# A hybrid attention and mixture-of-experts layer: the per-layer products moved into the first attention tile, and the extra blocks' tables made in parts inside expert blocks one to six

## The chip, the cores and the metric

The kernel runs on one core of one Trainium2 chip. The metric is the device time of one execution in microseconds (us), lower is better. Times of the kernel before: a median of 1537.45 us over three runs (1536.6 to 1537.8).

## The reference

One decoder layer on 512 tokens of width 1024, all in float32:

```python
h = x
a = rms_norm(h, g_mix);  proj = a @ w_in
o_moba = moba_attention(...)              # 8 heads of 64, causal, blocks of 256
o_gla  = rms_norm(gla_chunked(...), g_gla_norm) * silu(rg)
h = h + concat(o_moba, o_gla) @ w_out
f = rms_norm(h, g_ffn)
h = h + moe_ffn(f, w_router, b_router, w1, b1, w2, b2)   # top 4 of 32 experts
ple = rms_norm(p @ w_ple_proj, g_ple)     # p: 512 x 256, w_ple_proj: 256 x 1024
h = h + sigmoid(h @ w_ple_gate) * ple
return rms_norm(h, g_final)
```

An expert is `clamped_swiglu(x @ w1[e] + b1[e]) @ w2[e] + b2[e]`, with w1[e] 1024 x 2048 and w2[e] 1024 x 1024, so 12 MB of weights for each of 32 experts. `ple` depends on nothing but p and the weights: it can be computed at any time before the last sum.

## The kernel before, in words

Each engine has its own program, written out by hand in the order in which it runs; a program goes on when the semaphores it waits for have been counted up. Four token tiles of 128 (T0 to T3) go through these stages.

1. **Projection** (to about 162 us): `x` is normed and multiplied by w_in.
2. **Attention tiles** (about 162 to 282 us): a loop over t = 0 to 3, written out, with steps j = 0 to 5 for pairs of heads. In a tile PE computes the linear-attention products (L1058, L1106, L1108), the scores (L1070), transposes of the probabilities (L1098), and their product with v (L1082). From tile 1 on, the product with w_out for the tile before (`mix_out`, L1023) is filled in between. ACT does the exponentials (L729), copies the transposed probabilities (`pt_copy`, L737) and squares h for the norm (`h_square`, L745); DVE masks, scales, adds; POOL takes the powers (L571).
3. **Routing** (about 283 to 316 us): `mix_out` for T3, half n=0 and then half n=1, the router's logits (L1042, L1467), each token's four experts, ranks within an expert, the table `row_of` of 96 rows for each expert (L1650), and the gather of the first expert's rows from DRAM (POOL, L583).
4. **Experts**: blocks 0 to 31 of 96 rows, one for each expert, and then as many extra blocks as experts with more than 96 tokens need (their number n is read from a table at run time; in these inputs it is 0, as 31 adds of rows by L600 and 384 weight loads show). A block takes 12 pieces of weights of 1 MB each (k = 0 to 11). For each piece SP loads it into one of six slots (`load_chunk`, L411), ACT rounds it to the upper part (`split_hi`, L782), DVE subtracts that from it to get the lower part (`split_lo`, L1531; both into a ring of four pieces, `HL`), and PE multiplies upper and lower parts in 24 products of 128x512 (`w1_chunk` L1217, `w2_chunk` L1249). `turn_x` (L1205) transposes the gathered rows; ACT and DVE split those too (`split_x` L823, `rest_x` L1527), and w1 cannot begin before. `split_lo` counts up `w_lo`, on which SP waits before it fills the slot again. Piece 6 goes into the slot of piece 0. Block 0 is written out and takes its pieces in the order 0, 1, 2, 3, 8, 6, 7, 9, 10, 11; the others are one loop.
5. **Tail**: the gate product with w_ple_gate, `pleo`, last norm, store.

What the change touches lies in stages 2 to 4:

- **The per-layer products**: `turn_ple` (8 transposes, L1151) and `ple_tile` (L1180: 4 tiles x 2 halves x 2 products of 128x512 in float32, each shown as two matmuls) are issued on PE between the routing and block 0's pieces; ACT squares (L804) and scales (L808) the result from PSUM into `pleo`, POOL takes the power. SP loads their inputs (L461, L462) once seven halves of `mix_out` are done.
- **First weights**: SP loads pieces 0 and 1 right after the second half of w_out (with 2 and 3 at 273 us), ACT's `split_hi` of 0 to 3 stands ahead of `h_square(3)`, DVE's `split_lo(0, 0)` stands in the routing.
- **SP's order in the routing**: the load of piece 6 waits for `w_lo` 1, and behind it in SP's program stand the four loads of b1 (L467). ACT's rounding of b1 (`bb_hi`, L796) waits for these, and ACT's `split_x(0)` stands behind it.
- **Tables**: DVE L1674 to L1710 makes tables for all 53 possible blocks in block 0, PE multiplies them with one-hot rows (`gate_tables`, L1194, 16 products with 74 columns), and the loops of all engines begin with a wait for `tab_ready` and a load of n.

```python
            for k in range(4):
                split_hi(0, k)
            h_square(NT - 1)
            store_f(NT - 1)
```

## Time and profile before

| | |
|---|---|
| median of three runs | 1537.45 us |
| the profiled execution | 1536.28 us |
| its span in the trace | 1534.1 us |
| PE busy | 1494.5 us, 97% of the span |
| DVE busy | 1280.0 us, 83% |
| ACT busy | 1004.8 us, 65% |
| POOL busy | 198.5 us, 13% |
| PE's part of the chain that ended last | 94% |
| mean granted clock of PE | 0.988 |

PE, DVE, ACT, POOL are the engines for matrix products, vectors, activations and general work; SP issues DMAs. A busy PE is not PE at its peak, since matmul ends are modelled. The profiled execution is 1.2 us under the median of the runs.

### The profile page before, as it was taken

To read this page: it belongs to the slowest core of one execution; us is meant where nothing else is said; L and a number is where in the kernel's file an instruction comes from. 1 tells how busy PE (TensorE), PEld (TensorE's weight loads), DVE (VectorE), ACT (ScalarE), POOL (GpSimd) and SP (SyncE) were. 2 spreads that over 40 slices of the span, in tenths; PEclk is the share of its full clock that TensorE was granted. 3 is DMA by queue.
4 is the path that set the end of the run, shared out by engine and by line. 5 is a ranking of instruction groups with operands and counts; after the bars stand their busy time and mean duration, and the time that the engine had idled before them with its cause. 6 is when DMAs were issued, how large, how long until landed. Compare 5 with 4: busy or idle time off the path is not lost.

```text
span 1534.1 us, 20725 instructions
## 1 busy us (share of the span) xinstructions
PE 1494.5 (97%) x7115; PEld 1041.7 (68%) x7115; DVE 1280.0 (83%) x1109; ACT 1004.8 (65%) x919; POOL 198.5 (13%) x148
## 2 busy tenths in 40 slices
PE   7999899999999999999999999999999999999997
PEld 5878555566666666676666666666666666666666
DVE  5322356689999999999999999999999999999974
ACT  5432333457777777777777777777777777777642
POOL 6000000020211111111111121111111111111000
PEclk9999799989999999999999999999999999999999
DMA  5215400459999999999999999999999999999921
GB/s 171 98 67 192 178 15 14 157 188 355 374 393 370 372 376 381 375 379 381 380 382 376 377 377 370 375 372 387 373 384 376 382 381 375 380 376 367 380 100 55
DMA packets 126384, 466.58 MB, mean 304 GB/s; under 512 B 7955, under 2 KB 8518, under 8 KB 126358
## 3 DMA queue, kind: packets, MB, share of 16 engines
q1 hardware_dynamic: 118432, 438.73, 75.5%
q0 software_dynamic: 7312, 25.40, 6.8%
q10 hardware_dynamic: 614, 2.11, 0.3%
q8 instruction: 16, 0.26, 0.1%
q14 instruction: 10, 0.08, 0.0%
HBM read 446.67 MB, written 19.53 MB: 304 GB/s over the span
## 4 chain that ended last, share of the span: by engine, by line
PE 94%; DVE 2%; issue 2%; ACT 2%; DMA 0%; POOL 0%; DVEq 0%; POOLq 0%; ACTq 0%
PE ps L1217 46%; PE ps L1249 23%; PE ps L1004 9%; PE ps L1023 3%; PE ps L1347 2%; PE ps L1205 1%; PE ps L1256 1%; PE ps L1232 1%; PE ps L1180 1%; PE ps L1082 1%; PE ps L1070 1%; PE ps L1098 1%; PE ps L1108 1%; PE ps L1042 0%; DMA b_all<-in_b_router_dram 0%
## 5 line engine op out<-in xcount | busy, mean ns | idle before, releaser
L1531 DVE TENSOR_TENSOR HL<-W,HL 128x2048 fp32r<-128x2048 f32 x384 | 881.7, 2321 | 43.2 <-ACT HL L782 40.5
L782 ACT ACTIVATE HL<-W 128x2048 fp32r<-128x2048 f32 x382 | 731.9, 1917 | 174.7 <-PE ps L1217 100.6
L1217 PE MATMUL ps<-HL,XTh 128*96 128x512 f32 x2048 | 563.5, 397 | 0.5 <-DVE XTl L1527 0.5
L1217 PEld LDWEIGHTS ps<-HL,XTh 128*96 128x96 f32 x2048 | 323.2, 162 | 132.9 <-issue 1.9
L1217 PE MATMUL ps<-HL,XTl 128*96 128x512 f32 x1024 | 319.7, 393 | 0.0
L1249 PE MATMUL ps<-HL,HIDTh 128*96 128x512 f32 x1024 | 280.9, 396 | 1.7 <-DVE HIDTl L1559 1.3
L1249 PEld LDWEIGHTS ps<-HL,HIDTh 128*96 128x96 f32 x1024 | 162.7, 161 | 81.8 <-issue 13.2
L1217 PEld LDWEIGHTS ps<-HL,XTl 128*96 128x96 f32 x1024 | 165.2, 161 | 70.5
L600 POOL DMA_INDIRECT y_sums<-actT,row_of x31 | 60.8, 1962 | 949.4 <-ACT actT L841 949.4
L1249 PE MATMUL ps<-HL,HIDTl 128*96 128x512 f32 x512 | 159.6, 393 | 0.0
L1249 PEld LDWEIGHTS ps<-HL,HIDTl 128*96 128x96 f32 x512 | 82.7, 161 | 35.3
L1392 DVE TENSOR_TENSOR PWl<-wst,PWh 128x1024 fp32r<-128x1024 f32 x24 | 29.0, 1223 | 69.0 <-ACT PWh L667 68.1
L583 POOL DMA_INDIRECT XG<-f_rows,row_of x33 | 83.6, 2534 | 17.3 <-DVE row_of L1650 8.2
L812 ACT ACTIVATE HIDTh<-ps 128x384 fp32r<-128x384 f32 x64 | 31.5, 492 | 61.3 <-PE ps L1256 61.1
L1023 PE MATMUL ps<-wst,actT 128*128 128x512 f32 x128 | 58.9, 603 | 0.0
L673 ACT ACTIVATE W<-ps 128x512 f32<-128x512 f32 x20 | 11.9, 594 | 65.2 <-PE ps L1004 65.2
L729 ACT ACTIVATE M<-M,nmax 128x128 f32<-128x128 f32 (+3 forms) x32 | 18.0, 561 | 46.3 <-DVE nmax L1500 46.2
L1555 DVE TENSOR_TENSOR HIDr<-T,SIG 96x512 f32<-96x512 f32 x64 | 44.0, 688 | 5.0
L1497 DVE SCALAR_TENSOR_TENSOR M<-dist,ps 128x128 f32<-128x128 f32 (+3 forms) x32 | 15.4, 483 | 36.7 <-PE ps L1070 27.9
L817 ACT ACTIVATE SIG<-T 96x512 f32<-96x512 f32 x64 | 40.0, 624 | 9.3 <-DVE T L1543 8.3
L823 ACT ACTIVATE XTh<-ps 128x768 fp32r<-128x768 f32 x32 | 26.0, 813 | 28.3 <-PE ps L1217 26.0
L1543 DVE TENSOR_SCALAR T<-ps 96x512 f32<-96x512 f32 x64 | 43.5, 679 | 1.0 <-PE ps L1217 1.0
(270 smaller groups left out, 1378.8 us busy)
## 6 DMA issues: line engine op xcount, KB each, us to landing
W<-in_w_dram SPq DMA_DIRECT2D x384, 1024.0 KB, 8.3
wst<-in_w_in_dram SPq DMA_DIRECT2D x6, 2048.0 KB, 8.6
H<-in_x_dram SPq DMA_DIRECT2D x8, 512.0 KB, 5.0
wst<-in_w_out_dram SPq DMA_DIRECT2D x2, 2048.0 KB, 10.9
W<-in_w_ple_gate_dram SPq DMA_DIRECT2D x4, 1024.0 KB, 7.7
y_sums<-M SPq DMA_DIRECT2D x1, 2688.0 KB, 15.5
f_rows<-M ACTq DMA_DIRECT2D x4, 512.0 KB, 2.6
out_dram<-TL SPq DMA_DIRECT2D x4, 512.0 KB, 2.6
```

The costliest lines, as they stand in the source:

```text
L583: pool.indirect_dma_start(XG[:], None, f_rows, bass.IndirectOffsetOnAxis(ap=row_of[:, b:b + 1].bitcast(U32), axis=0)).then_inc(xg_in, 16)
L600: pool.indirect_dma_start(y_sums, bass.IndirectOffsetOnAxis(ap=rows.bitcast(U32), axis=0), YR, None, compute_op=ALU.add).then_inc(y_added, 16)
L782: act.activation(HL[:, k % HRING, 0], w_slot(k), ACT.Copy).then_inc(w_hi, 1)
L812: act.activation(HIDTh[:, 4 * h:4 * h + 4], ps[:, 2 * h, 0:4 * CAP].rearrange("p (f j) -> p f j", f=4), ACT.Copy).then_inc(hth_out, 1)
L817: act.activation(SIG[:], T1[:], ACT.Sigmoid, scale=ALPHA).then_inc(sig_done, 1)
L1004: last = pe.matmul(ps[:, g % 4], l, r, start=(c == 0 and m == 0), stop=(c == NC - 1 and m == 2))
L1023: last = pe.matmul(ps[:, bank], actT[:, c, t * P:(t + 1) * P], wst[:, n, c], start=(c == first_c), stop=(c == last_c))
L1217: last = pe.matmul(ps[0:CAP, 2 * h + n], xt[:, c], HL[:, s, part, cc * 1024 + n * 512:cc * 1024 + (n + 1) * 512], start=(h == 0 and c == 0 ...
L1249: last = pe.matmul(ps[0:CAP, 4 + n], ht[:, f], HL[:, s, part, ff * 1024 + n * 512:ff * 1024 + (n + 1) * 512], start=(f == 0 and ht is HIDT ...
L1531: dve.tensor_tensor(HL[:, k % HRING, 1], w_slot(k if ready is None else k - 4), HL[:, k % HRING, 0].bitcast(F32), ALU.subtract).then_inc(w ...
L1543: dve.tensor_scalar(t1, ps[0:CAP, 2 * h:2 * h + 2, 0:512:2], LIMIT, None, ALU.min).then_inc(glu_min, 1)
L1555: dve.tensor_tensor(HIDr[:, h * 512:(h + 1) * 512], T2[:], SIG[:], ALU.mult).then_inc(hid_ready, 1)
```

## The change

The inputs of the per-layer products, and `pleo`, get other places in SBUF: `pleo` takes the first 4096 columns of `W`, which were weight slots 0 and 1, and these slots move to a new area `W01`, which lies over the second half of w_out. So pieces 0 and 1 are loaded once the last tile's product with that half is done; to have it done first, the last tile takes half n=1 before n=0. The products are issued in tile 0, two halves per step. ACT copies them out in tile 0, squares them in tile 1, scales them in tile 2. `gate_tables` covers only the 32 first blocks in block 0; the tables of the extra blocks are made by DVE in six parts, in blocks 1 to 6, written out; PE multiplies them in block 6. The loops of PE, ACT and DVE are cut around block 6 and before block 31, and n is read only there.

```diff
+LATE = 6
-        wpp = wst[:, 0, 0:4, :]...
-        prow = wst[:, 0, 4:6, :]...
-        pT = wst[:, 0, 6:8, :]
-        pleo = wst[:, 1, :, :]...
+        wpp = in_w(18432, 2, D)
+        prow = in_w(20480, NT, PLE)
+        pT = in_w(21504, 2, SEQ)
+        pleo = in_w(0, NT, D)
...
-            return W[:, s * 2048:(s + 1) * 2048] if s < 4 else W45[:, s - 4]
+            return W01[:, s] if s < 2 else W[:, s * 2048:(s + 1) * 2048] if s < 4 else W45[:, s - 4]
...
         def extra_count(eng):
+            eng.wait_ge(tab_ready, 1)
...  (SP)
                 if n == 0:
                     sp.wait_ge(p_lo, 24)
+                    sp.wait_ge(st_ready, 14)
+                    sp.wait_ge(kt_ready, 2)
+                    sp.dma_start(wpp, w_ple_proj[0]...).then_inc(ple_ld, 16)
+                    sp.dma_start(prow, p[0, 0]...).then_inc(ple_ld, 16)
...
-            for k in range(2):
-                load_chunk(sp, 0, k, 0)
             sp.wait_ge(s_done, NT * MH)
             for k in range(2, 4):
                 load_chunk(sp, 0, k, 0)
             sp.wait_ge(wo_done, 2 * NT - 1)
-            sp.dma_start(wpp, ...)
-            sp.dma_start(prow, ...)
+            for k in range(2):
+                load_chunk(sp, 0, k, 0)
             sp.wait_ge(w_lo, 1)
             load_chunk(sp, 0, 6, 0)
             sp.wait_ge(lg_done, NT)
...
-            sp.wait_ge(pp_done, NT)
             for k in range(10, NK):
                 load_chunk(sp, 0, k, 0)
...  (ACT)
+            def ple_out(j):
+                if j == 0:
+                    for c in range(2):
+                        act.wait_ge(pt2_done, c + 1)
+                        act.activation(pT[:, c], ps[:, 3 - c], ACT.Copy).then_inc(pt2_out, 1)
+                else:
+                    for i in (2 * j - 2, 2 * j - 1):
+                        act.wait_ge(pp_done, i + 1)
+                        act.activation(pleo[:, i // 2, ...], ps[:, 3 - i % 2], ACT.Copy).then_inc(pp_out, 1)
...
                         if j < MH // 2:
                             expo(t * MH + i)
+                    if t == 0:
+                        ple_out(j)
                     for i in (2 * j - 2, 2 * j - 1):
                         if j >= 1:
                             pt_copy(t * MH + i)
+                    if t == 1 and j < NT:
+                        ple_square(j)
+                    if t == 2 and j < NT:
+                        ple_scale(j)
...
             with act.Fori(1, 2) as b:
                 expert_block(b, True)
-            act.wait_ge(tab_ready, 1)
+            with act.Fori(2, LATE) as b:
+                expert_block(b)
+            expert_block(LATE, late=True)
+            with act.Fori(LATE + 1, NE - 1) as b:
+                expert_block(b)
             n = extra_count(act)
-            with act.Fori(0, n + (NE - 2)) as i:
-                expert_block(i + 2)
+            with act.Fori(0, n + 1) as i:
+                expert_block(i + (NE - 1))
...  (PE)
+                    if t == 0 and j == 0:
+                        turn_ple()
+                    elif t == 0 and j <= MH // 2:
+                        ple_half(2 * j - 2)
+                        ple_half(2 * j - 1)
...
+            def extra_tables():
+                pe.wait_ge(gate_oh, 1)
+                for a in range(A):
+                    last = pe.matmul(ps[0:CAP, 6, 0:2 * NEXTRA], ohX[:, a, :], tables[:, a, :], ...)
+                last.then_inc(slot_gates, 1)
...  (DVE)
-            split_lo(0, 0)
-            half_turned(T3, 0, 2 * T3 + 1)
-            add_mix(T3, 1, 4)
-            half_turned(T3, 1, 2 * T3 + 2)
+            half_turned(T3, 1, 2 * T3 + 1)
+            add_mix(T3, 0, 4, 2 * T3 + 2)
+            half_turned(T3, 0, 2 * T3 + 2)
...
             dve.wait_ge(x_asked, 1)
+            split_lo(0, 0)
             split_lo(0, 1)
...
+            for b, part in enumerate((extra_experts, taken_blocks, block_tables, slots_hot, extra_pairs, extra_rows)):
+                expert_block(b + 1, part)
+            with dve.Fori(LATE + 1, NE - 1) as b:
+                expert_block(b)
```

Where instructions stand, at three places on which the prediction rests. PE's program in the first attention tile, from its second pair of scores to the second transposes of probabilities: L1070 and L1105 are the scores, L1098 and L1138 the transposes, L1069 and L1080 the per-layer transposes and products, the 64x128 rows and L1108 or L1148 linear attention, the rest the product with v. Before:

```order
L1070 MATMUL ps<-W 128x128 [waits s_masked]
L1070 MATMUL ps<-W 128x128
L1098 MATMUL ps<-ident,M 128x128 [waits p_scaled] x2
L1106 MATMUL ps<-M,W 64x128 [waits a_out]
```

And now:

```order
L1069 MATMUL ps<-ident,W 128x128 [waits ple_ld]
L1069 MATMUL ps<-ident,W 128x128 x7
L1105 MATMUL ps<-W 128x128 [waits s_masked]
L1105 MATMUL ps<-W 128x128
L1080 MATMUL ps<-W 128x512 [waits pt2_out]
L1080 MATMUL ps<-W 128x512 x3
L1138 MATMUL ps<-ident,M 128x128 [waits p_scaled] x2
L1146 MATMUL ps<-M,W 64x128 [waits a_out]
```

Eight transposes and four wide products stand ahead of the first transposes of probabilities; twelve more products stand ahead of the later ones. SP's program from the loads of w_out to b1, before:

```order
L453 DMA wst<-in_w_out_dram 128x8x512
L411 DMA W<-in_w_dram 128x2x1024 x2
L411 DMA W<-in_w_dram 128x2x1024 [waits s_done]
L411 DMA W<-in_w_dram 128x2x1024
L461 DMA wst<-in_w_ple_proj_dram 128x2x1024 [waits wo_done]
L462 DMA wst<-in_p_dram 128x4x256
L411 DMA W<-in_w_dram 128x2x1024 [waits w_lo]
L467 DMA actT<-in_b_dram 32x512 [waits lg_done]
```

And now:

```order
L466 DMA wst<-in_w_out_dram 128x8x512
L418 DMA W<-in_w_dram 128x2x1024 [waits s_done]
L418 DMA W<-in_w_dram 128x2x1024
L418 DMA W<-in_w_dram 128x2x1024 [waits wo_done]
L418 DMA W<-in_w_dram 128x2x1024
L418 DMA W<-in_w_dram 128x2x1024 [waits w_lo]
L478 DMA actT<-in_b_dram 32x512 [waits lg_done]
```

Pieces 0 and 1 now come after pieces 2 and 3, behind the wait for `wo_done`; the loads of b1 still stand behind piece 6 and its wait for `w_lo`. ACT's program there, now (L814 is `split_hi` of pieces 0 to 3, L771 `h_square`, L825 the rounding of b1, L840 `split_x`):

```order
L814 ACTIVATE HL<-W 128x2048 [waits w_slot_in0]
L814 ACTIVATE HL<-W 128x2048 [waits w_slot_in1]
L814 ACTIVATE HL<-W 128x2048 [waits w_slot_in2]
L814 ACTIVATE HL<-W 128x2048 [waits w_slot_in3]
L771 ACTIVATE M,ss<-H 128x1024 [waits f_stored,h_ready]
L775 DMA f_rows<-M 128x1024 [waits f_ready]
L821 ACTIVATE ex<-ex 128x16 [waits e_in]
L823 ACT_TABLE_LOAD
L823 ACTIVATE gcol<-tok 96x1
L825 ACTIVATE BB<-actT 128x512 [waits bias_in]
L840 ACTIVATE XTh<-ps 128x768 [waits xt_done]
```

These rows stand in the same order as before, apart from two copies of the per-layer transposes, which are gone from behind the DMA. And DVE's program, now, from the table `row_of` to block 0's second pieces (L1560 is `split_lo`, L1696 the lower part of b1, L1556 `rest_x`):

```order
L1680 SCALAR_TENSOR_TENSOR row_of<-ps,none 96x32 [waits dve_step]
L1685 TENSOR_REDUCE s<-ex 128x4 [waits e_out]
...
L1560 TENSOR_TENSOR HL<-W,HL 128x2048 [waits w_hi,x_asked,dve_step]
L1560 TENSOR_TENSOR HL<-W,HL 128x2048 [waits w_hi]
L1696 TENSOR_TENSOR BB<-actT,BB 128x512 [waits bb_hi]
L1556 TENSOR_TENSOR XTl<-ps,XTh 128x768 [waits xh_ready]
L1560 TENSOR_TENSOR HL<-W,HL 128x2048 [waits w_hi] x2
```

Before, only one `split_lo` stood between the wait for `x_asked` and the lower part of b1; the one of piece 0, which counts `w_lo` to 1, has moved here from the routing.

## Rows read from the trace of the kernel before

**Rows 1.** The page, part 4: the chain that ended last, share of the span by engine.

```profile
PE 94%; DVE 2%; issue 2%; ACT 2%; DMA 0%; POOL 0%; DVEq 0%; POOLq 0%; ACTq 0%
```

**Rows 2.** Stretches of one block: us, busy of PE, PEld, DVE, ACT, POOL, clock, DMA, GB/s.

```profile
574.28:609.72 35.44, 35.44 (x170) 24.68 (x169) 34.24 (x24) 27.02 (x21) 5.45 (x3) 1.00 1.02 378
1212.20:1247.64 35.44, 35.44 (x170) 24.68 (x169) 33.55 (x24) 26.84 (x21) 4.35 (x2) 1.00 1.02 379
```

**Rows 3.** A stretch of 1 us in the first attention tile, columns as in rows 2.

```profile
166.00:167.00 1.00, 0.12 (x2) 0.00 (x0) 0.78 (x4) 0.32 (x3) 0.00 (x0) 0.50 0.86 352
```

**Rows 4.** Chain of waits: start us, us, what; the first two attention tiles.

```profile
167.73 0.69 PE ps L1098 x2
...
183.92 1.94 PE ps L1058 x8
...
194.82 0.37 PE ps L1106 x4
195.19 0.42 PE ps L1108 x2
```

**Rows 5.** Chain of waits: per-layer products (L1180), first pieces, tables (L1194).

```profile
311.94 3.67 PE ps L1180 x4
...
321.45 2.76 PE ps L1217 x12
324.22 3.63 PE ps L1180 x8
...
330.62 3.43 PE ps L1180 x8
...
343.86 2.70 PE ps L1194 x32
```

**Rows 6.** Timeline of PE, a run of products with 32 columns.

```profile
303.39 1.01 PE L1145 MATMUL ps<-M 128*96 128x32 f32 x10
```

**Rows 7.** Timeline of ACT: start us, us, operation, idle before and releaser.

```profile
208.91 1.06 ACT L745 ACTIVATE M<-H 128x1024 f32<-128x1024 f32 x1
...
318.06 1.02 ACT L804 ACTIVATE wst<-ps 128x1024 f32<-128x1024 f32 x1 [0.94 <-PE ps L1180]
```

**Rows 8.** DMA issues from 273.0 to 273.45, from 273.45 and from 300: us to landing last.

```profile
W<-in_w_dram SPq DMA_DIRECT2D x2, 1024.0 KB, 8.0
...
W<-in_w_dram SPq DMA_DIRECT2D x1, 1024.0 KB, 9.0
...
actT<-in_b_dram SPq DMA_DIRECT2D x4, 64.0 KB, 2.8
```

**Rows 9.** Timeline, all engines, the routing.

```profile
282.94 7.30 ACT L782 ACTIVATE HL<-W 128x2048 fp32r<-128x2048 f32 x4
...
291.65 0.37 SPq L461 DMA_DIRECT2D wst<-in_w_ple_proj_dram  x1
...
300.13 1.06 ACT L745 ACTIVATE M<-H 128x1024 f32<-128x1024 f32 x1 [9.89 <-DVE H L1449]
...
303.59 2.11 SPq L467 DMA_DIRECT2D actT<-in_b_dram  x4
```

**Rows 10.** Timelines of POOL, DVE and PE, from the first gather to block 1.

```profile
310.44 1.11 POOL L583 DMA_INDIRECT XG<-f_rows,row_of  x1 [8.22 <-DVE row_of L1650]
...
312.03 0.17 DVE L1655 TENSOR_REDUCE s<-ex 128x4 f32<-128x16 f32 x1 [1.87 <-ACT ex L792]
...
314.03 2.29 DVE L1531 TENSOR_TENSOR HL<-W,HL 128x2048 fp32r<-128x2048 f32 x1
...
317.15 0.96 DVE L1527 TENSOR_TENSOR XTl<-ps,XTh 128x768 fp32r<-128x768 f32 x1 [0.23 <-ACT XTh L823]
...
323.09 0.86 DVE L1674 TENSOR_TENSOR M<-it_b,xend 128x672 f32<-128x672 f32 x1
...
315.45 0.83 PE L1205 MATMUL ps<-ident,XG 96*128 96x96 f32 x8
...
361.64 1.17 PE L1217 MATMUL ps<-HL,XTh 128*96 128x512 f32 x4 [0.45 <-DVE XTl L1527]
```

More of the change, by code:

```diff
@@ L589, in _ @@
             pool.tensor_tensor(asked[:], tok[0:1, 0:1], tok[0:1, 0:1], ALU.add).then_inc(x_asked, 1)
[L590 to L596 removed]
+            gather(1)
             def add_rows(rows):
@@ L787, in _ @@
             store_f(NT - 1)
-            for c in range(2):
-                act.wait_ge(pt2_done, c + 1)
-                act.activation(pT[:, c], ps[:, 4 + c], ACT.Copy).then_inc(pt2_out, 1)
             act.wait_ge(e_in, 1)
@@ L841, in store_y, with expert_block @@
                     act.activation(YR[:, i * 512:(i + 1) * 512], ps[0:CAP, 4 + i], ACT.Copy, scale=gcol[:]).then_inc(yr_out, 1)
-            def expert_block(b, second=False):
+            def expert_block(b, second=False, late=False):
                 split_hi(b, 0)
@@ L847, in expert_block @@
                 sigmoid(b - 1, 1)
+                if late:
+                    act.wait_ge(slot_gates, 2)
+                    act.activation(slot_gate[:, NE:NBLK + NEXTRA], ps[0:CAP, 6, 0:2 * NEXTRA], ACT.Copy).then_inc(slot_gates_out, 1)
                 split_hi(b, 2)
@@ L1047, in _, with turn_ple, ple_half @@
             pe.wait_ge(consts, 17)
+            def turn_ple():
+                pe.wait_ge(ple_ld, 32)
+                for c in range(2):
+                    for t in range(NT):
+                        last = pe.transpose(ps[:, 3 - c, t * P:(t + 1) * P], prow[:, t, c * P:(c + 1) * P], ident[:])
+                    last.then_inc(pt2_done, 1)
+            def ple_half(i):
+                if i == 0:
+                    pe.wait_ge(pt2_out, 2)
+                elif i >= 2:
+                    pe.wait_ge(pp_out, i - 1)
+                t, n = i // 2, i % 2
+                for c in range(2):
+                    last = pe.matmul(ps[:, 3 - i % 2], pT[:, c, t * P:(t + 1) * P], wpp[:, c, n * 512:(n + 1) * 512],
+                                     start=(c == 0), stop=(c == 1))
+                last.then_inc(pp_done, 1)
             MIX_STEPS = [range(0, 5), range(5, 8), range(8, 13), range(13, 16)] + 2 * [range(0)]
@@ L1147, in slot_tokens @@
                     last.then_inc(tok_done, 1)
-            def turn_ple(c):
-                for t in range(NT):
-                    last = pe.transpose(ps[:, 4 + c, t * P:(t + 1) * P], prow[:, t, c * P:(c + 1) * P], ident[:])
-                last.then_inc(pt2_done, 1)
             pe.wait_ge(oh_ready, 1)
@@ L1199, in gate_tables, with turn_x @@
                 last.then_inc(gt_done, 1)
-            def turn_x(b):
+            def extra_tables():
+                pe.wait_ge(gate_oh, 1)
+                for a in range(A):
+                    last = pe.matmul(ps[0:CAP, 6, 0:2 * NEXTRA], ohX[:, a, :], tables[:, a, :], start=(a == 0), stop=(a == A - 1))
+                last.then_inc(slot_gates, 1)
+            def turn_x(b, late=False):
+                if late:
+                    pe.wait_ge(slot_gates_out, 2)
                 pe.wait_ge(xg_in, b * 16 + 16)
@@ L1581, in expert_block @@
                 split_lo(b, 5)
+                if part is not None:
+                    part()
                 second_half(b)
@@ L1679, in _ @@
-            link(dve.tensor_scalar(tabf[:, NBLK:NBLK + 1], xend[:, NE - 1:NE], 0.0, None, ALU.add))
-            link(dve.tensor_copy(tab[:], tabf[0:1, :]))
-            link(dve.tensor_scalar(full, Jm, CAP - 0.5, None, ALU.is_gt))
-            link(dve.tensor_copy(has, full))
-            for j in range(2, MAXFULL + 1):
-                link(dve.scalar_tensor_tensor(out=full, in0=Jm, scalar=j * CAP - 0.5, in1=full, op0=ALU.is_gt, op1=ALU.add))
-            link(dve.scalar_tensor_tensor(out=Jm, in0=full, scalar=-float(CAP), in1=Jm, op0=ALU.mult, op1=ALU.add))
@@ L1709, in _ @@
-            link(dve.tensor_reduce(own[:], has[:, 0], AX.X, ALU.add))
-            link(dve.tensor_scalar(pair[:, NE:NBLK], tabf[:, NE:NBLK], own[:, 0:1], None, ALU.is_equal))
             split_lo(0, 6)
             clamp(0, 0)
+            dve.wait_ge(slot_gates, 1)
             swiglu(0, 0)
```

216 lines of the change are left out of this document (102 added, 114 removed).

## The prediction, made before the run

> **What bounds the kernel now.** I read the page first: PE holds 94% of the chain that ended last [rows 1]. Then the stretches of one expert block: 35.44 us each, PE busy for all of it at the full clock, DVE for 33.55 to 34.24 us [rows 2]. So the 31 looped blocks run at PE's rate, and DVE has only 1.2 to 1.9 us of room in each. Nothing in the change makes a looped block shorter; what it can win lies before block 1, which begins at 361.64 us [rows 10]. There the chain of waits shows the per-layer products on PE's path: 3.67 us ahead of the first expert's rows, 5.18 us that the chain has between those rows and the first piece at 321.45, and 3.63 and 3.43 us between pieces [rows 5]. The reader is to see that this work fills PE while others are waited for: the first piece of weights is used at 321.45, while the split rows were begun at 317.15 and took 0.96 [rows 10].
>
> **Tile 0 takes the products in.** Sixteen products of 3.43/4 = 0.86 us at the full clock make 13.7 us [rows 5]. Before, this tile is full of short waits, and PE's clock fell to half (1.2 GHz) in it [rows 3]; its last matmul is followed by the next tile at 183.92 [rows 4]. Step by step, now: the eight transposes lie in the wait between the first two pairs of scores. The first product needs ACT's two copies of them (0.6 each), which stand behind two exponentials that end at about 166.1, so it starts at about 167.3, where before the first transposes of probabilities stood (167.73) [rows 4]. From there PE has hardly a wait left: 13.7 us of products; linear attention at the full clock 4 x (0.37 + 0.42) = 3.2 us [rows 4]; other small work at the full clock about 3.4 (an estimate: the rows of tile 0, such as 0.69 for two transposes, at 0.6 of their length); one last copy 0.6. The clock was half when it started; the four products at 311.94, which met the same, took 3.67 instead of 1.71 us, so 2.0 us for that [rows 5]. Sum: 167.3 + 13.7 + 3.2 + 3.4 + 0.6 + 2.0 = 190.2, against 183.9: **+6.3**. The next tile's first products (1.94 us at half clock [rows 4]) then run at the full clock, which gives 1.0 back: **+5.3**. Bounds: +3.3 without any half clock, and +22 if it stays half through the whole tile (17 us more for the products and the rest).
>
> **Tiles 1 and 2.** ACT squares (1.02 plus 0.2 to read the sum) and scales (about 1.1) one tile of the products in each of steps 0 to 3 [rows 7]. Three of four lie where ACT waits for PE. The one of step 3 stands right ahead of `h_square`, which before began with no wait behind `pt_copy` at 208.91 and is on the chain to the next tile [rows 7]: **+1.2 and +1.1**. Bounds: 0, and 9.3 if all eight showed. The power on POOL and the mean on DVE are once for four tiles and hidden.
>
> **The late first weights.** Pieces 0 and 1 used to be in place long before. Now SP issues them where the per-layer inputs were issued, 291.65 [rows 9]. Pieces 2 and 3, the nearest row, issued as a pair like this one, took 8.0 in the median and 9.0 for the second [rows 8]: piece 1 lands at about 292.1 + 9.0 = 301.1. ACT works in its own order, and `split_hi` of pieces 0 to 3 (7.30 for four, so 1.8 each [rows 9]) stands ahead of `h_square(3)`. Pieces 1, 2 and 3 end at 301.1 + 5.4 = 306.5; before, `h_square(3)` started at 300.13, released by DVE [rows 9]. The norm, the last logits, the ranks and the table of rows follow it without slack, so the first gather goes from 310.44 to about 316.8: **+6.4**. Lower bound +4.1, if both landed 5.5 us after 291.65 and all four splits ran then (297.0 + 7.3).
>
> **The wait for b1 behind it.** `split_lo(0, 0)` now follows the gather. Before, the wait for ACT (1.87) stood in DVE's way, and the first split began at 314.03 [rows 10]; without that wait and 6.4 later it is at 318.6, and `w_lo` is 1 at 320.9. Only then does SP issue piece 6 and the four loads of b1, which took 2.11 us to issue and 2.8 to land, at 303.59, long before they were needed [rows 8, 9]. Now they land at about 320.9 + 0.4 + 2.1 + 2.8 = 326.2. ACT's rounding of b1 (0.6) and `split_x` (0.8) and DVE's `rest_x` (0.96 [rows 10]) come behind: PE begins the first piece at about **329.2**, against 321.45 [rows 5]. Were the gather alone in charge, it would be 318.1 + 6.4 = 324.5.
>
> **Block 0.** From the first piece to block 1 it took 361.64 - 321.45 = 40.2 us, PE being busy throughout; without 3.63 and 3.43 of products it is 33.1 [rows 5, 10]. PE will have waited most of the time since the routing when it starts, so 2.0 us for half clock again. `gate_tables` has 32 instead of 74 columns but still 32 matmuls; 32 took 2.70 us, 0.084 each [rows 5], and with 32 columns 10 took 1.01, 0.10 each [rows 6], so I count no gain. Block 1 at 329.2 + 33.1 + 2.0 + 0.1 = 364.4: **+2.8**. DVE, which loses most of its tables here, is no bound; at most piece 8, whose load waits for `w_lo` 3, comes 1 to 2 us late. Lower bound: gather alone in charge, +4.1 for the weights and no half clock: 322.2 + 33.1 = 355.3, -6.3.
>
> The Trainium skill says on the table's width ("TensorE: Matmul & The Clock Gate", LDWEIGHTS) that loading the stationary operand takes its column count over 1.2 GHz, here 96/1.2 = 80 ns whatever the moving width; by it a narrow table and the second table in block 6 each cost 2.6 us, and by columns alone 1.2 and 1.5 us. The trace agrees with the rule (84 ns at 74 columns, 100 at 32), and it speaks against splitting the table in two.
>
> **Blocks 1 to 31.** PE multiplies the extra tables in block 6: the same 32 matmuls, **+2.7** [rows 5], with nothing to hide in, since PE is full. DVE's six parts: the first has an operation of 0.86 [rows 10], a reduction as long and some small ones, 2.6 us as an estimate, and the others 0.5 to 2.2. Room is 1.9 a block, 1.2 while POOL scales the products [rows 2], and DVE is only just ahead when block 1 starts (PE waited 0.45 for it at 361.64 [rows 10]). The first four parts overdraw it by 0.3 to 0.7 each, 2.3 together, of which I put **+1.0** on PE; bounds 0 and 3. The read of n before block 31 and the cut loops: 0, hidden by queued work as at 361.64; at worst 1.
>
> **Sum.** 5.3 + 2.3 + 2.8 + 2.7 + 1.0 = **+14.1 us** on the profiled execution's 1536.3, so 1550.4. The median of the runs stands 1.2 above that execution, so I predict 1551.5 us.
>
> **Rivals.**
>
> 1. *The first expert starts when its rows are there* (faster). If pieces 0 and 1 land so soon, and b1 too, that `h_square(3)` and `split_x(0)` keep their time, PE starts at 318.1 and reaches block 1 at 318.1 + 33.1 = 351.2, -10.4. With tile 0 at its lower bound (+3.3) and block 6 (+2.7) the sum is -4.4: 1533 us. For it: ACT had 9.89 us of waiting ahead of `h_square` [rows 9]. Against: the second piece would have to land by 294.7, 2.6 us after its issue, and nothing of 1 MB did. It decides when what tile 0 to 2 and the blocks cost stays under 10.4. Chance 0.09.
> 2. *The costs fall at their lower ends* (no change). Tile 0 at +3.3, nothing in tiles 1 and 2, block 1 at -4, block 6 +2.7: +2, 1539.5 us. For it: DVE's first block is lighter. Chance 0.08.
> 3. *My forecast.* Late weights and b1 behind `w_lo` take back what the moved products free, and tile 0 pays for them: 1551.5. Chance 0.70.
> 4. *The clock stays half through tile 0.* The bound of +22 instead of +5.3: 1568 us. For it: before, the half clock of 166 us still held when the next tile began at 183.92 [rows 3, 4]. Against: that tile had small products; the wide ones at 311.94 brought the clock up. Chance 0.13.
>
> **How the numbers follow.** A measurement of this kernel tells about 0.2%, 3.1 us, from no change. Faster by more: rival 1, 0.09. Within: rival 2, 0.08. Slower: 0.83. The likeliest is 1551.5. The range goes down to 1541, which leaves out rivals 1 and nearly all of 2, and up to 1564, into rival 4, whose clock may come back late in the tile: the bounds of my own terms (-4 for tiles 0 to 2, -9 for block 0 but not together with them, +3 for DVE) lie within.
>
> **What would show it.** In the trace after: tile 1 starts at 189 to 191 us, not 184, with a half clock that ends within some 4 us of the first product; `h_square(3)` starts 14 us later than 300.13 (7.6 from the tiles, 6.4 from the weights), and the split ahead of it waits for a DMA of weights; ACT waits for the DMA of b1 ahead of `split_x(0)`; the first piece is used at about 337, block 1 at 372; the blocks stay 35.44 us but block 6, which has 2.7 more, and some of 1 to 4. I am wrong if block 1 starts before 361 us, or if looped blocks change their length.

## The result: slower by 28.7 us, twice the forecast

The changed kernel took 1566.3 us (median of 4 runs, 1563.2 to 1566.8), the kernel before in the same comparison 1537.6 (1536.6 to 1539.1): a ratio of 1.0182, 95% interval 1.0164 to 1.0199. The prediction was 1551.5 with a range of 1541 to 1564. The direction was right, the size was not. The span of the profiled execution grew by 30.7, from 1534.1 to 1564.8 us.

**The profile after.** First the page: busy time (part 1), the chain that ended last by engine (part 4) and two groups of part 5.

```profile
PE 1503.3 (96%) x7147; PEld 1046.3 (67%) x7147; DVE 1275.4 (82%) x1102; ACT 1005.9 (64%) x928; POOL 214.2 (14%) x141
...
PE 73%; DVE 3%; issue 1%; DMA 1%; POOL 1%; ACT 1%; SPq 0%; POOLq 0%; ACTq 0%; DVEq 0%
...
L1242 PE MATMUL ps<-HL,XTh 128*96 128x512 f32 x2048 | 566.8, 398 | 12.4 <-DVE XTl L1556 8.2
...
L608 POOL DMA_INDIRECT y_sums<-actT,row_of x31 | 77.6, 2503 | 942.6 <-ACT actT L858 942.6
```

The chain of this profile is followed back to 320.9 us only, and its row adds up to about 80%, so the 73% are not to be set against the 94% of [rows 1]. Three of its pieces (start us, us, what) are new: the landing of b1, an add of POOL's and a gather.

```profile
334.88 5.31 DMA actT<-in_b_dram
...
402.51 10.98 POOL y_sums L608
413.80 10.77 DMA XG<-f_rows,row_of
```

PE is busy for 96% of the span, so the question is where PE stands still or runs slower. The sum by stages is read from PE's and ACT's timelines of both profiles. A block's rows are turned in the block before it, so "rows of block 3" is a mark inside block 2.

| mark | before | after | later by | new |
|---|---|---|---|---|
| tile 0 begins | 162.60 | 166.13 | 3.5 | 3.5 |
| tile 1 begins | 183.85 | 194.07 | 10.2 | 6.7 |
| `h_square(2)` | 278.19 | 290.48 | 12.3 | 2.1 |
| rows of block 2 turned | 370.40 | 387.12 | 16.7 | 4.4 |
| rows of block 3 | 405.82 | 424.62 | 18.8 | 2.1 |
| rows of block 6 | 512.15 | 531.18 | 19.0 | 0.2 |
| rows of block 7 | 547.59 | 575.97 | 28.4 | 9.4 |
| rows of the last block | 1433.59 | 1463.47 | 29.9 | 1.5 |
| end | 1534.1 | 1564.8 | 30.7 | 0.8 |

**Tile 0.** PE's timeline (start us, us, line, operation, count, idle before and releaser), the counterpart of [rows 4]:

```profile
166.13 1.16 PE L1093 MATMUL ps<-W 128*128 128x128 f32 x8 [1.18 <-ACT W L732]
...
170.68 3.70 PE L1080 MATMUL ps<-W 128*128 128x512 f32 x8 [1.32 <-ACT W L751]
...
178.47 3.70 PE L1080 MATMUL ps<-W 128*128 128x512 f32 x8
...
194.07 1.16 PE L1093 MATMUL ps<-W 128*128 128x128 f32 x8
```

Four such groups, 14.8 us of products (14.2 from start to start, as ends are modelled), and between them hardly a wait: PE is the bound of the tile, which takes 27.9 us and not 21.25. The clock, half in this tile before [rows 3], is granted in full from 166 to 194 us, so tile 1's first eight take 1.16 and not 1.94 us. It was full already before the first product at 170.68.

**The first expert.** The timelines of ACT and PE, for [rows 5, 9, 10]:

```profile
311.03 1.91 ACT L814 ACTIVATE HL<-W 128x2048 fp32r<-128x2048 f32 x1 [15.70 <-DMA W<-in_w_dram]
...
318.93 1.04 ACT L771 ACTIVATE M<-H 128x1024 f32<-128x1024 f32 x1
...
340.21 0.63 ACT L825 ACTIVATE BB<-actT 128x512 fp32r<-128x512 f32 x1 [11.89 <-DMA actT<-in_b_dram]
```

```profile
333.31 1.51 PE L1230 MATMUL ps<-ident,XG 96*128 96x96 f32 x8 [5.30 <-DMA XG<-f_rows,row_of]
...
342.67 1.99 PE L1242 MATMUL ps<-HL,XTh 128*96 128x512 f32 x4 [7.85 <-DVE XTl L1556]
```

Both forecast waits are there: ACT waits 15.70 us for piece 0 and comes to `h_square(3)` 18.8 us later than before, 6.5 more than `h_square(2)`; and it waits 11.89 for b1, while the first expert's rows are long there.

**Block 2 and block 6**, which I had not forecast. POOL's timeline from block 1 into block 2, and below PE's, ACT's and DVE's. After:

```profile
402.51 10.98 POOL L608 DMA_INDIRECT y_sums<-actT,row_of  x1 [46.82 <-ACT actT L858]
413.80 3.99 POOL L597 DMA_INDIRECT XG<-f_rows,row_of  x1 [0.30 <-issue]
```

The same two on POOL in the kernel before:

```profile
384.09 5.30 POOL L600 DMA_INDIRECT y_sums<-actT,row_of  x1 [44.15 <-ACT actT L841]
389.70 2.02 POOL L583 DMA_INDIRECT XG<-f_rows,row_of  x1 [0.30 <-issue]
```

With the change, PE in block 2, then PE, ACT and DVE in block 6:

```profile
424.62 0.88 PE L1230 MATMUL ps<-ident,XG 96*128 96x96 f32 x8 [1.45 <-DMA XG<-f_rows,row_of]
```

```profile
563.55 2.83 PE L1221 MATMUL ps<-tables,actT 128*96 128x42 f32 x32
566.21 0.53 PE L1281 MATMUL ps<-ident,HIDr 96*128 96x96 f32 x4
570.80 2.02 PE L1242 MATMUL ps<-HL,XTh 128*96 128x512 f32 x4 [4.06 <-DVE HL L1560]
```

```profile
566.42 0.20 ACT L867 ACTIVATE slot_gate<-ps 96x42 f32<-96x42 f32 x1 [10.46 <-PE ps L1221]
```

```profile
568.45 6.70 DVE L1560 TENSOR_TENSOR HL<-W,HL 128x2048 fp32r<-128x2048 f32 x3 [8.17 <-ACT HL L814]
```

In block 6 ACT, in its order, stands 10.46 us at the copy of a table that PE has not yet made; the splits of pieces 2 to 4 are queued behind it, DVE waits 8.17 us for them, and PE runs out of weights and drops to half clock (granted 0.50 from 570 to 574 us; 2.02 us for four matmuls that take 1.1 otherwise). On the way into block 2 an add that took 5.30 us before takes 10.98, and the gather of block 3's rows is queued behind it.

**All other blocks.** Two rows of PE's timeline, one block apart:

```profile
1143.97 0.82 PE L1230 MATMUL ps<-ident,XG 96*128 96x96 f32 x8
1179.47 0.82 PE L1230 MATMUL ps<-ident,XG 96*128 96x96 f32 x8
```

35.50 us and not 35.44 [rows 2], in every looped block.

### The profile page after: what moved, and what is told of

The parts are those of the page before. It is cut to its first block, busy times and chain, and to the rows that moved or that the text cites. A ratio compares the mean times of both kernels' runs of the same rounds, so it can differ in the third digit from the quotient of the medians.

```text
span 1564.8 us, 20411 instructions
## 1 busy us (share of the span) xinstructions
PE 1503.3 (96%) x7147; PEld 1046.3 (67%) x7147; DVE 1275.4 (82%) x1102; ACT 1005.9 (64%) x928; POOL 214.2 (14%) x141
## 4 chain that ended last, share of the span: by engine, by line
PE 73%; DVE 3%; issue 1%; DMA 1%; POOL 1%; ACT 1%; SPq 0%; POOLq 0%; ACTq 0%; DVEq 0%
PE ps L1242 44%; PE ps L1274 22%; PE ps L1373 2%; DVE HL L1560 2%; PE ps L1230 1%; PE ps L1257 1%; PE ps L1281 1%; POOL y_sums L608 1%; DMA XG<-f_rows,row_of 1%; PE ps L1340 0%; ACT HL L814 0%; DMA actT<-in_b_dram 0%; PE ps L1353 0%; PE ps L1221 0%; PE ps L1211 0%
## 5 line engine op out<-in xcount | busy, mean ns | idle before, releaser
L1560 DVE TENSOR_TENSOR HL<-W,HL 128x2048 fp32r<-128x2048 f32 x384 | 881.3, 2319 | 51.0 <-ACT HL L814 48.1
L814 ACT ACTIVATE HL<-W 128x2048 fp32r<-128x2048 f32 x382 | 730.4, 1913 | 198.2 <-PE ps L1242 105.5
L608 POOL DMA_INDIRECT y_sums<-actT,row_of x31 | 77.6, 2503 | 942.6 <-ACT actT L858 942.6
L1579 DVE SCALAR_TENSOR_TENSOR T<-T 96x512 f32<-96x512 f32 x64 | 43.5, 680 | 3.1 <-PE ps L1211 3.0
```

Source lines behind the costliest of these rows:

```text
L608: pool.indirect_dma_start(y_sums, bass.IndirectOffsetOnAxis(ap=rows.bitcast(U32), axis=0), YR, None, compute_op=ALU.add).then_inc(y_added, 16)
L814: act.activation(HL[:, k % HRING, 0], w_slot(k), ACT.Copy).then_inc(w_hi, 1)
L1560: dve.tensor_tensor(HL[:, k % HRING, 1], w_slot(k if ready is None else k - 4), HL[:, k % HRING, 0].bitcast(F32), ALU.subtract).then_inc(w ...
L1579: dve.scalar_tensor_tensor(out=T2[:], in0=T2[:], scalar=1.0, in1=T1[:], op0=ALU.add, op1=ALU.mult).then_inc(moe_step, 1)
```

## Experiments

### Three waits, one by one and together

e1 moves ACT's copy of the late table:

```diff
-                if late:
-                    act.wait_ge(slot_gates, 2)
-                    act.activation(slot_gate[:, NE:NBLK + NEXTRA], ...)
                 split_hi(b, 2)
                 choose_bias(b)
                 split_hi(b, 3)
                 split_hi(b, 4)
+                if late:
+                    act.wait_ge(slot_gates, 2)
+                    act.activation(slot_gate[:, NE:NBLK + NEXTRA], ...)
                 move_out(b - 1, 1)
```

> ACT's copy of the extra blocks' table out of PSUM in block 6 stands behind split_hi 4 of that block, ahead of move_out, instead of ahead of split_hi 2; everything else as in the changed kernel (1566.3 us). Theory A: block 6 takes 44.79 instead of 35.50 us because ACT waits 10.46 us for the product of the tables before it may split pieces 2 to 4, and PE then waits for the weights (4.06) with its clock at half. Without it block 6 takes 35.5 + 2.8 for the 32 matmuls = 38.3, so 6.5 less: 1560 us. Rival B: the block is long because PE has the 32 matmuls and DVE the sixth part in it, and the wait for the weights is DVE's lateness: then the time stays within 1 us of 1566.3.

Measured: 1559.2 us (1556.9 to 1561.0), ratio to before 1.0127 (1.0102 to 1.0151), 7.1 less than the changed kernel. Block 6 takes 38.20 us instead of 44.79, as A said. The row in the new profile:

```profile
567.26 0.20 ACT L871 ACTIVATE slot_gate<-ps 96x42 f32<-96x42 f32 x1 [3.46 <-PE ps L1221]
```

ACT still waits, 3.46 us, but with its splits done.

e2 moves SP's loads of the biases:

```diff
-            sp.wait_ge(w_lo, 1)
-            load_chunk(sp, 0, 6, 0)
             sp.wait_ge(lg_done, NT)
...
             sp.dma_start(b2s, b2[0]).then_inc(b2_in, 16)
+            sp.wait_ge(w_lo, 1)
+            load_chunk(sp, 0, 6, 0)
```

> SP issues the loads of b1 and b2 as soon as the last logits are there, ahead of its wait for w_lo 1 and of piece 6. Theory A: the first piece waits for them (342.67, where its rows are there at 333.31): now b1 lands at about 322 + 5.3 = 327.3, before those rows, and the first piece begins at 333.3 + 1.2 (transposes) + 0.8 (ACT) + 1.0 (DVE) = 336.3, 6.3 us earlier, and so does block 1: 1560 us. Rival B: what PE wins at the first piece it loses in block 0 to DVE (gate tables, piece 8 that is loaded later), so that block 1 starts 0 to 2 us earlier: 1564 to 1566 us.

Measured: 1557.7 us (1556.7 to 1564.1), ratio 1.0135 (1.0104 to 1.0166), 8.6 less. Some of that is the start of the run and a stretch of half clock in tile 1 (both below): from `h_square(2)` to the first piece it is 46.1 us instead of 52.2, so 6.1, and to the rows of block 2 5.8. A holds; nothing of it is lost in block 0. PE's wait at the first piece, of 7.85 us, is now:

```profile
332.59 1.99 PE L1242 MATMUL ps<-HL,XTh 128*96 128x512 f32 x4 [1.99 <-DVE XTl L1556]
```

e3 moves `h_square(3)` and `store_f(3)` ahead of the splits:

```diff
+            h_square(NT - 1)
+            store_f(NT - 1)
             for k in range(4):
                 split_hi(0, k)
-            h_square(NT - 1)
-            store_f(NT - 1)
```

> ACT's h_square(3) and store_f(3) stand ahead of its splits of pieces 0 to 3, as data needs them and not as before. Theory A: the late weights hold the norm of the last tile: h_square(3) starts when the last half of H is there, about 312.6 instead of 318.93, the first gather comes 6.3 us earlier (322.7), and the whole chain behind it, b1 included, since piece 0 is split by 316 all the same: 1560 us. Rival B: the splits of pieces 0 to 3 behind it then end at about 321 and hold ACT's exponential, DVE's split of piece 0 and so the loads of b1, and half or all of the 6.3 us is lost: 1563 to 1566 us.

Measured: 1561.5 us (1556.5 to 1564.1), ratio 1.0152 (1.0128 to 1.0176), 4.8 less. In the profile `h_square(3)` comes 21.9 instead of 28.5 us after `h_square(2)`, 6.5 as A said. The first piece comes 4.4 us earlier, block 2's rows 5.2: the loads of b1, which wait for the split of piece 0, take back 1 to 2 us, a part of B.

> The three edits together. Theory A: three separate waits, one behind the other on PE's path, so they add up: 6.5 + 6.3 + 6.3 = 19.1 us less, 1547 us, and what is left over the kernel before is tile 0 and the tiles behind it (8.8), the half clock at the start of the projection (3.5), the gather for block 3 (2.1), the products in block 6 (2.8) and 0.06 us in each block. Rival B: e2 and e3 overlap, since with the square first piece 0 is split later and the loads no longer depend on it: then DVE or the gather is the next wait, and the sum is 12 to 15 us, 1551 to 1554.

Measured: 1549.1 us (1545.8 to 1550.7), ratio 1.0061 (1.0040 to 1.0081), 17.2 less. From `h_square(2)` to block 2's rows 86.4 instead of 96.6 us, 10.3 less, where e2 and e3 alone gave 5.8 and 5.2: they nearly add up. It is now even less than the 92.2 of the kernel before, so the first expert does gain 5.9 us from the change, once these waits are gone.

### What tile 0 costs

e7 is e4 with `for c in range(2)` in `ple_half` cut to the first, so the output lacks the second half of that sum.

> e4_all_three, and the per-layer products in tile 0 take the first 128 of their 256 rows only, so 8 matmuls instead of 16; the other half of that sum is left out of the output. Theory A: in tile 0 PE has become the bound, so half of 4 x 3.70 us of products less is 6 to 7.4 us less on the whole: 1542 to 1543 us. Rival B: tile 0 is bound by its chain of waits with ACT and DVE, as before the change, with PE's clock at half when it has less to do: then half of the products gives 1 to 3 us, 1546 to 1548.

Measured: 1546.2 us (1543.3 to 1557.0), ratio 1.0058 (1.0031 to 1.0085). The median is 2.9 us under e4's, B's figure rather than A's, but it says little: the runs are 13.7 us apart, and the profiled one came to tile 0 at 170.40, 5.1 us later than e4's. The tile itself, PE's timeline:

```profile
170.40 1.16 PE L1092 MATMUL ps<-W 128*128 128x128 f32 x8 [1.17 <-ACT W L732]
...
174.94 1.98 PE L1079 MATMUL ps<-W 128*128 128x512 f32 x4 [1.32 <-ACT W L751]
...
191.99 1.16 PE L1092 MATMUL ps<-W 128*128 128x128 f32 x8
```

21.6 us instead of 27.9: 6.35 less for 6.9 us of products less. So PE is the bound of the tile, as A says, and the clock stays full with half of the products too (1.00 from 166 to 192 us).

### What the start of the run adds

> The kernel before, on this chip, for a second profile of it. Theory A: the half clock in the first projection (20 to 30 us from the start) and the 35.50 us of a looped block belong to the run and the chip, not to the change: here too the block may be 35.50 and the stretch 20 to 30 may show a granted clock under 1. Rival B: both belong to the change: blocks 35.44, clock 1.00.

Measured: 1538.5 us in one run. Stretches of 10 us (columns as in rows 2), of the kernel before, of the changed one, of e7 and of this second profile of before:

```profile
20.00:30.00 10.00, 9.30 (x37) 5.98 (x36) 6.79 (x9) 8.97 (x11) 8.86 (x13) 1.00 0.42 146
```

```profile
20.00:30.00 10.00, 9.30 (x23) 5.66 (x22) 6.11 (x9) 8.23 (x10) 9.01 (x12) 0.66 0.47 166
```

```profile
20.00:30.00 10.00, 9.32 (x31) 4.02 (x29) 8.31 (x12) 8.50 (x11) 8.71 (x15) 0.86 0.09 13
30.00:40.00 10.00, 10.00 (x37) 8.01 (x36) 5.61 (x6) 4.00 (x4) 4.59 (x9) 0.80 0.53 199
```

```profile
20.00:30.00 10.00, 9.29 (x29) 5.80 (x28) 6.59 (x10) 9.04 (x10) 9.01 (x12) 0.83 0.39 131
```

The clock at which PE begins the projection differs between profiles, of one kernel too: tile 0 begins at 162.6 and 164.5 in the two profiles of before, and from 162.4 (e17) to 170.4 (e7) in those with the change. So I put the 3.5 us of the first line of the table, all but 0.6 (below), down to the run. That the change has no part in them is not shown: the four profiles with the longest half clock there (the changed kernel, e1, e7, e12) are all of kernels with the change, which has 12 of the 19 profiles. The looped block is 35.44 us here: that part of A is refuted.

A second stretch of this kind lies in tile 1. The changed kernel's profile and, below it, e5's:

```profile
220.00:230.00 10.00, 7.91 (x48) 5.64 (x46) 6.00 (x13) 3.38 (x9) 1.57 (x2) 0.83 0.14 56
```

```profile
220.00:230.00 10.00, 7.91 (x48) 5.32 (x48) 6.17 (x14) 4.15 (x9) 1.57 (x2) 1.00 0.14 56
```

From tile 1 to `h_square(2)` it is 96.4 us in the five profiles with that half clock (the changed kernel, e4, e6, e7, e13) and 94.84 in the seven others with the change.

### The gathers of blocks 2 to 7

e5 issues block 3's gather ahead of block 0's add:

```diff
-                gather(b + 2)
+                if b != 1:
+                    gather(b + 2)
+                if b == 0:
+                    gather(3)
                 add_block(b)
```

> e4_all_three, and POOL issues the gather of block 3's rows ahead of its add of block 0's outputs, not behind it. Theory A: the rows of block 3 come late because POOL's add of block 0 takes 10.98 us and the gather stands behind it, so that block 2 is 37.66 instead of 35.50 us from transposes to transposes. With the gather out first that is gone: 2.1 us less than e4_all_three (1549.1), 1547 us, and the add may take as long as it likes. Rival B: the gather is late because POOL as such is slow there, so a gather issued earlier takes the 11 us itself, or PE then waits for something else: 0 to 1 us less.

Measured: 1547.1 us (1546.2 to 1548.6), ratio 1.0049 (1.0032 to 1.0065). Block 3's rows come 35.9 instead of 37.7 us after block 2's, but block 4's 37.0 after them, since its gather stands behind the second add. Together the two give 0.35 us less: B, the wait moved on by a block. The rest between the two profiles is e4's half clock in tile 1, 1.6 us, less 0.4 by which e5 comes to tile 0 later.

e6 has `LATE = 7` and DVE's parts in blocks 2 to 7.

> e4_all_three, and DVE's six parts stand in blocks 2 to 7 and PE's product of the extra tables in block 7, not in 1 to 6. Theory A: POOL's add takes 10.98 instead of 5.30 us because DVE, with the first part in block 1, has no pause while POOL writes its descriptors. Without a part in block 1 the add takes about 5.3 and block 2 is 35.5: 2 us less than e4_all_three, 1547 us. Rival B: DVE comes out of block 0 so late that it has no pause in blocks 1 and 2 without a part either: add and stall stay as they are, 1549 us.

Measured: 1564.2 us (1562.4 to 1565.5), ratio 1.0157 (1.0140 to 1.0174), 15.1 more than e4. In block 1 A is right: without a part of DVE's in the block the add takes 2.96 us. Then, in block 4, timelines of POOL and PE:

```profile
497.63 10.87 POOL L608 DMA_INDIRECT y_sums<-actT,row_of  x1 [24.82 <-ACT actT L858]
508.02 4.59 POOL L623 TENSOR_TENSOR W<-W,actT 128x256 f32<-128x256 f32 x1
512.77 14.35 POOL L597 DMA_INDIRECT XG<-f_rows,row_of  x1 [0.16 <-issue]
```

```profile
533.82 1.54 PE L1230 MATMUL ps<-ident,XG 96*128 96x96 f32 x8 [14.51 <-DMA XG<-f_rows,row_of]
```

Add, scaling and gather, 5.9 us together in a looped block of the kernel before, take 29.8 with DVE busy throughout, and PE stands 14.5 us. The Trainium skill ("SBUF — State Buffer", SBUF: two separate sides) says that a DMA of GpSimd's queue has its descriptors written by GpSimd, and that VectorE can lock it out of a port they share, so that the DMA only appears to be slow. The trace agrees as to who is slow: it is POOL's own instruction that takes 14.35 us. No row shows the port itself. What the rows show is DVE's pause: between 370 and 700 us in the profiles of before, the changed kernel, e6, e11 and e13, every add of 1.8 to 2.4 us has one of 0.5 to 1.04 us in it, and every longer add, from 2.95 to 10.98 us, has none over 0.2. The gathers of 2.8 us have none either, so a busy DVE does not by itself make a gather slow; what else it takes is open.

e11 is e4 with the parts in blocks 3, 5, 7, 9, 11 and 13.

> e4_all_three (1549.1), and DVE's six parts stand in blocks 3, 5, 7, 9, 11 and 13, PE's product of the extra tables in block 13. Theory A: POOL's adds and gathers take long where DVE never pauses, and a part of the tables takes DVE's pauses of its block and, while it is behind, of the next. With a free block between two parts DVE catches up (1.5 us of room in each), the adds take 1.9 to 5.5 us, and no block but 13 is longer than 35.5: 2.2 us less than e4_all_three, 1547. Rival B: DVE does not catch up in one block, or each part alone starves POOL: then a gather is late in some of these blocks as in e6_parts_one_later, where it cost 14.5 us in one: 1549 to 1565.

Measured: 1560.1 us (1558.8 to 1575.4), ratio 1.0181 (1.0122 to 1.0240). B: with the first part in block 3 the add of 457.06 takes 10.82 us, the gather of 472.20 12.69, and the next block takes 49.0. So one part alone can starve POOL. The parts in blocks 5, 7 and 9, where POOL scales too, lengthen adds to 5.6 to 5.9 us, but no gather, and PE does not wait.

e12 adds to e11 the new place of the two tiles, the order of exponential and splits on ACT, and of b1's rest on DVE.

> e11_parts_spaced, with fa and ha in a part of actT that is free then (so the other tiles lie as in the kernel before), ACT's exponential of the gates between its splits of pieces 1 and 2, and DVE's rest of b1 ahead of its split of piece 1. Theory A: the small tiles cost what e9 is to show, 2.5 to 3.3 us, and the two orders 1.1 us at the first piece: with the 2.2 of e11 about 6 us less than e4_all_three: 1543, still over before by tile 0 (6.7 to 8.8) less what the first expert gains. Rival B: the place of the tiles does nothing: step 0.2314 here too, and 1546 us.

Measured: 1573.1 us (1571.0 to 1574.8), ratio 1.0232 (1.0201 to 1.0262): two blocks of 48 us instead of one, behind the parts in blocks 3 and 5. But two parts of A hold: the other blocks are 35.44 us, and from `h_square(3)` to the first piece it is 18.2 instead of 19.4.

e13 has the parts back in blocks 1 to 6 and every gather ahead of the add:

```diff
-                if b + 2 == NE:
-                    pool.wait_ge(tab_ready, 1)
-                gather(b + 2)
+                if b == 0:
+                    gather(2)
+                if b + 3 == NE:
+                    pool.wait_ge(tab_ready, 1)
+                if b + 3 <= NE:
+                    gather(b + 3)
                 add_block(b)
```

> e12_best_try with DVE's parts back in blocks 1 to 6, and POOL's gather of block b+3 ahead of its add of block b in every block (e5 had it for block 3 only). Theory A: what PE waits for in blocks 2 to 7 is a gather that stands behind an add (up to 10.98 us) and a scaling (up to 4.6) of a starved POOL, though its buffer has been free for 14 us by then. Issued as soon as the buffer is free it lands in time even if it takes 12.7 us: every block but 6 is 35.44 us, block 6 38.2. From e4_all_three (1549.1): 2.2 for the gather, 2.3 for the tiles' place, 1.2 for the first piece: 1543. Rival B: a starved gather holds up the add behind it, and ACT, which waits for the add before it writes the next outputs, holds its splits: a block or two are longer by some us: 1546 to 1560.

Measured: 1542.4 us (1538.9 to 1543.9), ratio 1.0027 (1.0015 to 1.0039). POOL is as slow as ever:

```profile
375.27 4.46 POOL L597 DMA_INDIRECT XG<-f_rows,row_of  x1 [33.05 <-PE ps L1235]
389.59 10.98 POOL L608 DMA_INDIRECT y_sums<-actT,row_of  x1 [9.86 <-ACT actT L863]
...
482.02 11.66 POOL L597 DMA_INDIRECT XG<-f_rows,row_of  x1 [6.86 <-PE ps L1235]
```

and PE waits for no gather: 35.44 us from block 3 on, 38.14 for block 6. It was the order of gather and add, on a POOL that is slow while DVE has no pause; theory A, but for block 2, which still takes 35.87.

### 128 bytes

All profiles of kernels with the change's two new tiles show a product of the projection, lines that it does not touch, every 0.2314 us (from start to start, the mean of the stretch 40 to 110 us), both of before every 0.2304.

```diff
+        fa = sb("fa", [P, NT * TOPK])
+        ha = sb("ha", [P, NT * TOPK])
         row_of = sb("row_of", [CAP, NTAB], I32)
```

> The kernel before, with the two small tiles fa and ha (64 bytes of each partition each) allocated at the place where the change allocates them, and used by nothing: all tiles behind them lie 128 bytes further on. In the profiles of all changed kernels the products of the projection, lines that the change does not touch, follow each other every 0.2314 us, in both profiles of the kernel before every 0.2304, and a looped block takes 35.50 instead of 35.44. Theory A: the place of the tiles does it: here the step is 0.2314 and the block 35.50 us, and the time 0.06 x 31 + 0.001 x 600 + 0.8 for the tail = 3.3 us over before: 1541 to 1542. Rival B: it is the programs (loops, queues) of the change: step 0.2304, block 35.44, time as before within its scatter of 2 us.

Measured: 1539.8 us (1538.7 to 1542.1), ratio 1.0015 (1.0002 to 1.0029), and in the profile step 0.2314 and the looped blocks 35.50, to the hundredth as in the changed kernel. PE's timeline:

```profile
1080.28 0.82 PE L1207 MATMUL ps<-ident,XG 96*128 96x96 f32 x8
1115.78 0.82 PE L1207 MATMUL ps<-ident,XG 96*128 96x96 f32 x8
```

From the last block's rows to the end it is 101.3 us here and in the changed kernel, 100.5 before: the 0.8 of the tail too. The ratio makes it 2.3 us over before, with an interval from 0.3 to 4.5, against A's 3.3.

> The kernel before with one tile of 64 bytes added where e9_two_tiles_added had two. Theory A: it is where the tiles begin modulo 128 or more that decides: with 64 bytes the step of the projection's products differs from 0.2304 too, 0.2314 or more. Rival B: it is the 128 bytes alone: 0.2304. For a looped block 35.44 and 35.50.

> The kernel before with one tile of 256 bytes added at that place. Theory A: places that are a multiple of 256 bytes apart are alike, and 128 is between two of them: step 0.2304, block 35.44. Rival B: any move of the tiles costs the same: 0.2314 and 35.50.

> The kernel before with one unused tile of 32 bytes at that place. Theory A: the step depends on where in some unit of 128 or 256 bytes the tiles begin, and 32 bytes lie between 0 (0.2304) and 64 (0.2267): a step between these two. Rival B: only multiples of 64 bytes are good places: step over 0.2304.

70 us of the projection in the kernels before, e9 (128 bytes), e14 (64), e15 (256) and e18 (32), in this order; the count of matmuls stands behind PE's busy time:

```profile
40.00:110.00 70.00, 70.00 (x306) 57.05 (x305) 20.25 (x21) 25.52 (x31) 0.00 (x0) 1.00 0.26 90
```

```profile
40.00:110.00 70.00, 70.00 (x304) 56.83 (x303) 20.57 (x21) 25.81 (x31) 0.00 (x0) 1.00 0.26 90
```

```profile
40.00:110.00 70.00, 70.00 (x311) 57.95 (x310) 19.94 (x20) 25.27 (x30) 0.00 (x0) 1.00 0.26 90
```

```profile
40.00:110.00 70.00, 70.00 (x306) 57.04 (x305) 19.96 (x20) 24.40 (x29) 0.00 (x0) 1.00 0.26 90
```

```profile
40.00:110.00 70.00, 70.00 (x305) 56.87 (x304) 20.32 (x21) 25.59 (x31) 0.00 (x0) 1.00 0.26 90
```

Steps of 0.2304, 0.2314, 0.2267, 0.2304 and 0.2311; blocks of 35.44, 35.50, 35.39, 35.44, and for 32 bytes 35.42 to 35.57 in turn. One run each took 1533.8 (64 bytes), 1538.2 (256) and 1538.2 us (32). So 0 and 256 are alike, as A of e15 said, and 64 is the best place of the five. Other than A of e14 said, its step is shorter and not longer. 32 does not lie between its neighbours, and B's rule for it, that multiples of 64 are good, fails at 128. Which tile matters is open.

> e14_one_tile_64 again, the kernel before with one unused tile of 64 bytes, now timed. Theory A: the place of the tiles sets the step of the products (0.2267 instead of 0.2304 us in the projection, block 35.39 instead of 35.44), so it is faster than before by 0.0037 x 600 for the projection + 0.05 x 31 for the blocks + what the tail gives, 4 to 5 us: 1533.5 to 1534.5 against 1538.3. Rival B: one look by chance: within 2 us of before.

Measured: 1533.1 us (1532.1 to 1533.6), ratio 0.9963 (0.9950 to 0.9977). **The kernel before with one unused tile of 64 bytes beats both kernels.**

> e13_gather_ahead_all (1542.4) with the same unused tile of 64 bytes. Theory A: the gain of the place adds to the rest of the change undone or not: step 0.2267, block 35.39, 4 us less: 1538, equal to the kernel before and 4 over e16. Rival B: 64 bytes do other things with the change's own tiles (W01, tables) moved: no gain, 1542.

Measured: 1536.8 us (1535.4 to 1541.6), ratio 0.9994 (0.9982 to 1.0006), 3.7 over e16. Step and block are those of e16, so A holds. The change with its waits mended gains 7.9 us from `h_square(2)` to block 2's rows (84.25 against 92.10), and pays 7.8 from tile 0's beginning to `h_square(2)` (122.77 against 114.97), 2.7 in block 6 and 0.5 in block 2: 3.1 us, and the two spans are 3.0 apart (1534.5 and 1531.5).

## Why the prediction was wrong, step by step

- **Tile 0 takes the products in (+5.3), tiles 1 and 2 (+2.3): right.** From tile 0's beginning to `h_square(2)` it is 124.35 instead of 115.59 us, +8.8 against +7.6; in e1, e2, e3 and e5 122.8, +7.2. That tile 0 comes out right is partly luck. No half clock came, so rival 4 fails altogether, and so do the 2.0 us for it in my sum; the products made up 0.5 of that (14.2 from start to start, not 13.7), and most of the rest PE's short waits for ACT (0.39, 0.81 and 0.56, where I had one copy of 0.6). Tiles 1 and 2 pay little: from tile 1 to `h_square(2)` 94.84 in those four profiles, 94.34 before. In this profile it is 96.41, by the half clock in tile 1, and that is what makes the 8.8.
- **The late first weights (+6.4): right**, 6.5; with `h_square(3)` ahead of the splits (e3) they are gone.
- **The wait for b1 and block 0 (+2.8 in all): right in kind, 1.6 short.** The mis-sized term is the landing of b1: 5.3 us, behind piece 6, which I took as 2.8 from a row where no weights were being loaded. Ahead of piece 6 it lands in 2.0 (e2) and 2.9 us (e4). e2 shows that this wait cost 6.1.
- **Block 6 (+2.7): the step that failed.** It costs 9.3 (44.79 over 35.50). I priced PE's 32 matmuls and called them the whole cost; they are (e1: 38.20 us, 2.70 over 35.50). I did not ask what is queued behind ACT's new wait for their result. ACT works ahead of PE, so it stands there 10.46 us, and 6.6 us more come out on PE. e1 shows it.
- **DVE's parts (+1.0, bounds 0 to 3): inside the bounds, by luck, on a wrong path.** 2.3 us come from them, but in blocks 2 to 5 PE never waited for DVE: with its pauses gone POOL was slow, and a gather was behind an add. In e6 the same cause costs 14.5, beyond any bound I had.
- **Blocks 1 to 31 keep their 35.44 us, reading n 0: the first wrong.** 35.50, with 0.6 in the projection and 0.8 in the tail some 2.9 us in all by the profiles, by the place of the tiles (e9, whose runs give 2.3). I had named that as what would make me wrong, but no rival for it.
- **The span against the median.** 2.9 of the 30.7 us (3.5 less the 0.6) I put down to the half clock at the start of this run; that the change has no part in it is not shown. The medians are 28.7 apart.

14.1 forecast, 6.6 for ACT's wait, 1.3 for the gather, 2.9 for the place, 1.6 for b1, 1.2 for the tiles (the half clock in tile 1) and 2.9 for the start make 30.6 of 30.7.

## What to carry to other kernels

When a piece of work moves into the middle of a full pipeline, price for each engine the wait that its result brings, not only the work: an engine that runs ahead (ACT here, by 10 us) loses its lead, and so does all that it has queued behind. Put a gather as soon as its buffer is free, ahead of stores that can wait: here one of 11.66 us then cost PE nothing. And an added tile, however small, moves all tiles behind it: compare the step of lines that were not touched before explaining a difference of a few tenths of a per cent, and try a few offsets, since one of them may be the cheapest gain of all.
